# One fused transformer block: head 0's expert indices alone and early, two weight rooms for gathered rows, top-k with 112 sums and 16-bit decoding

## The reference, cut to what matters

```python
q = (xt @ w_query).reshape(T, PEER_HEADS, PEER_KEY_DIM)          # 256 x 8 heads x 256
s1 = einsum('thd,hkd->thk', q[..., :128], sub_keys_1)            # 128 scores a head
s2 = einsum('thd,hkd->thk', q[..., 128:], sub_keys_2)
v1, i1 = lax.top_k(s1, 16); v2, i2 = lax.top_k(s2, 16)
cand = v1[..., :, None] + v2[..., None, :]                       # 16 x 16 sums
top_s, pos = lax.top_k(cand.reshape(..., 256), 16)
eidx = i1[pos // 16] * 128 + i2[pos % 16]                        # 128 experts a token
g = softmax(top_s)
a = gelu(einsum('cd,ced->ce', x, expert_down[eidx]))             # gathered rows of 8 KB
out = einsum('ce,ced->cd', a * g, expert_up[eidx])
```

## Time and profile before

| | |
|---|---|
| three runs | 1957.28, 1952.40, 1950.53 us; median 1952.4 |
| the profiled execution | 1953.55 us, of which the span of the program is 1951.8 |
| busy over the span | PE 93%, DVE 77%, ACT 44%, POOL 29% |
| moved by DMA | 620.26 MB, mean 318 GB/s; gathers 336.11 MB, SP's queue 280.05 MB |
| mean granted clock of PE | 0.979 of full speed |

### The profile page before, as it was taken

The page is one execution under the profiler, slowest core; times in us unless marked ns, Lnnn a source line. Parts: engine busy times, 40 slices in busy tenths (PEclk is TensorE's granted clock), DMA queues, the critical chain, the costliest instruction groups (busy, mean ns, idle before and its releaser), DMA issues.

```text
span 1951.8 us, 26465 instructions
## 1 busy us (share of the span) xinstructions
PE 1814.4 (93%) x10535; PEld 1500.8 (77%) x10535; DVE 1498.7 (77%) x2001; ACT 856.5 (44%) x1262; POOL 566.3 (29%) x369
## 2 busy tenths in 40 slices
PE   8999999999999989979989857679999999999997
PEld 7979987888899879968788744467767776777765
DVE  5354447444456556999999999999989999899888
ACT  4333336444433343323333289864344433344344
POOL 1302300000000000556567668842332113222221
PEclk9999999999999999989999989989999999999999
DMA  7864550355556644899999999989999999999996
GB/s 261 299 226 146 174 170 22 125 179 192 184 182 225 237 162 163 312 426 426 419 426 425 422 372 405 422 362 414 421 426 427 427 427 428 427 428 427 427 427 239
DMA packets 142677, 620.26 MB, mean 318 GB/s; under 512 B 9680, under 2 KB 20192, under 8 KB 84464
## 3 DMA queue, kind: packets, MB, share of 16 engines
q0 software_dynamic: 46352, 336.11, 41.5%
q1 hardware_dynamic: 93712, 280.05, 38.5%
q10 hardware_dynamic: 2512, 2.75, 0.4%
HBM read 616.77 MB, written 2.10 MB: 317 GB/s over the span
## 4 chain that ended last, share of the span: by engine, by line
PE 55%; DVE 23%; DMA 11%; issue 6%; ACT 3%; POOL 1%; SPq 0%; DVEq 0%; ACTq 0%
PE psum L679 54%; DVE down_rows L2306 11%; DMA u_raw<-in_peer_expert_up_dram 10%; POOL down_rows L1359 1%; DVE u_lo L2438 1%; DVE late_sum L2459 1%; ACT u_hi L1814 1%; DVE w_lo L1945 1%; DMA down_rows<-in_peer_expert_down_dram,eidx 1%; DMA x_in<-in_x_dram 0%; PE psum L697 0%; DVE late_rows L2306 0%; DVE onehot L2258 0%; DVE onehot L2261 0%; DVE key L2263 0%
## 5 line engine op out<-in xcount | busy, mean ns | idle before, releaser
L1945 DVE TENSOR_TENSOR w_lo<-raw,w_hi 128x2048 fp32r<-128x2048 f32 x124 | 286.1, 2307 | 337.6 <-ACT w_hi L1460 337.5
L1359 POOL DMA_INDIRECT down_rows<-in_peer_expert_down_dram,eidx x155 | 274.5, 1771 | 630.2 <-DVE eidx L2267 550.5
L1460 ACT CAST w_hi<-raw 128x2048 fp32r<-128x2048 f32 x124 | 236.6, 1908 | 397.4 <-PE psum L679 397.3
L679 PE MATMUL psum<-act_both,w_hi 128*128 128x256 f32 (+1 forms) x1664 | 390.1, 320 | 0.0
L1814 ACT CAST u_hi<-u_raw 128x2048 fp32r<-128x2048 f32 x112 | 214.3, 1913 | 359.7 <-DMA u_raw<-in_peer_expert_up_dram 354.3
L679 PE MATMUL psum<-act_both,w_lo 128*128 128x256 f32 x1088 | 307.0, 282 | 0.0
L679 PEld LDWEIGHTS psum<-act_both,w_hi 128*128 128x128 f32 x1664 | 276.1, 191 | 24.6 <-issue 0.6
L2438 DVE TENSOR_TENSOR u_lo<-u_raw,u_hi 128x2048 fp32r<-128x2048 f32 x112 | 256.5, 2290 | 0.0
L679 PEld LDWEIGHTS psum<-act_both,w_lo 128*128 128x128 f32 x1088 | 207.6, 191 | 0.0
L2306 DVE CUSTOM_DVE_ANT_0 down_rows<-down_rows,xn 128x2048 f32<-128x2048 f32 x91 | 205.4, 2288 | 0.6 <-DVE ind L2216 0.4
L679 PE MATMUL psum<-w_hi,act_both 128*128 128x512 f32 x640 | 201.5, 393 | 0.2 <-DVE w_lo L1945 0.2
(11 more groups left out here) (344 smaller groups left out, 3049.8 us busy)
## 6 DMA issues: line engine op xcount, KB each, us to landing
u_raw<-in_peer_expert_up_dram SPq DMA_DIRECT2D x128, 1024.0 KB, 11.9
raw<-in_w_in_dram SPq DMA_DIRECT2D x76, 1024.0 KB, 5.0
raw<-in_w_out_dram SPq DMA_DIRECT2D x16, 1024.0 KB, 5.0
raw<-in_peer_w_query_dram SPq DMA_DIRECT2D x16, 1024.0 KB, 5.0
raw<-in_w_up_nsa_dram SPq DMA_DIRECT2D x8, 1024.0 KB, 4.9
raw<-in_w_up_fox_dram SPq DMA_DIRECT2D x8, 1024.0 KB, 5.0
cmp_w<-in_k_cmp_w_dram SPq DMA_DIRECT2D x4, 1024.0 KB, 10.7
cmp_w<-in_v_cmp_w_dram SPq DMA_DIRECT2D x4, 1024.0 KB, 10.8
```

Of the source, the lines that this page charges most:

```text
L679: return nc.tensor.matmul(*a, skip_group_check=True, **k)
L1359: nc.gpsimd.indirect_dma_start(rows[:], None, table, bass.IndirectOffsetOnAxis(ap=eidx[:, half, slot:slot + 1], axis=0)).then_inc(landed, 16)
L1460: nc.scalar.copy(w_hi[:, p % 2], raw[:, p]).then_inc(hi_done, 1)
L1945: tt(w_lo[:, p % 2], raw[:, p], f32(w_hi[:, p % 2]), ALU.subtract).then_inc(lo_done, 1)
```

## The change

It has four parts.

- **Two weight rooms for the last blocks.** From block `RAW_PAIR` = 29 on the pieces use `raw[0]` and `raw[1]` only; a load waits for the low part two pieces back. Rooms 2 and 3 become free for gathered rows after block 28, and `order` and `ring` are changed to suit.
- **Head 0 alone.** Its sums and indices come in `topk_end(0, 0, 1)` after the low part of block 29's first piece, head 1's later, after block 30's third. `eidx_done` counts one more; POOL's first 16 slots wait for the first. Lists of heads 2 and 3 move behind the last low part and dot 4, the last `evac` behind dot 5; dots 0 to 2 come earlier.
- **112 sums.** Of the 16 x 16 sums only those of the first 4 rows (all columns) and the first 4 columns of the other 12 are made, two heads in one call.
- **Decoding in 16 bits.** Both lists are compared and multiplied in one operation each over 2 x 16 x 32 elements of 16 bits, followed by one reduction a head; the position is decoded with more small steps.

```diff
+RAW_PAIR = 29
+TOP_A, TOP_B = 4, 4
+NCAND = TOP_A * TOPK + (TOPK - TOP_A) * TOP_B
...
+        def index_sets(t):
+            return 1 if t < TOPK else t // (2 * TOPK) + 2
+        def raw_room(b, p):
+            return p % 2 if isinstance(b, int) and b >= RAW_PAIR else p
...
-        order = [8, 9, 10, 0, 8, 1, 9, 10, 4, 6, 2, 0, 3, 8, 1, 5, 7]
-        ring = [4, 6, 2, 0, 3, 1, 5, 7]
+        order = [8, 9, 10, 2, 3, 8, 9, 10, 4, 6, 0, 2, 1, 3, 8, 5, 7]
+        ring = [4, 6, 0, 2, 1, 3, 5, 7]
...
-                        sp.wait_ge(lo_done, 4 * (b - 1) + p + 1)
-                    sp.dma_start(raw[:, p], src(p)).then_inc(raw_loaded[p], 16)
+                        two = isinstance(b, int) and 4 * b + p >= 4 * RAW_PAIR + 2
+                        sp.wait_ge(lo_done, 4 * b + p - (1 if two else 3))
+                    r = raw_room(b, p)
+                    sp.dma_start(raw[:, r], src(p)).then_inc(raw_loaded[r], 16)
...
-                if slot % (2 * TOPK) == 0:
-                    pool.wait_ge(eidx_done, t // (2 * TOPK) + 1)
+                if t in (0, TOPK) or t and slot % (2 * TOPK) == 0:
+                    pool.wait_ge(eidx_done, index_sets(t))
...
+                elif r < 2:
+                    pool.wait_ge(lo_done, 4 * (NBLK - 1) + r + 3)
                 elif r < 4:
-                    pool.wait_ge(lo_done, 4 * (NBLK - 1) + r + 1)
+                    pool.wait_ge(lo_done, 4 * (RAW_PAIR - 1) + r + 1)
...
-            def top_sums(half, h):
+            def top_sums(half, h0, h1):
+                for c0, rows_, cols_ in ((0, slice(0, TOP_A), TOPK), (TOP_A * TOPK, slice(TOP_A, TOPK), TOP_B)):
+                    nr = rows_.stop - rows_.start
+                    seq(tt(cand[:, at_, c0:c0 + nr * cols_].rearrange("p n (a b) -> p n a b", a=nr),
+                           v1[:, :, rows_].unsqueeze(3).to_broadcast([P, nh, nr, cols_]),
+                           v2[:, :, 0:cols_].unsqueeze(2).to_broadcast([P, nh, nr, cols_]), ALU.add))
...
-                for l in range(2):
-                    seq(tt(oh, pabf[:, l, hs]..., iota, ALU.is_equal))
-                    seq(tt(eq, eq, indf[:, hs, l, :]..., ALU.mult))
-                    seq(V.tensor_reduce(key12[:, l, ks], oh, AX_X, ALU.add))
+                seq(tt(eq, rank16[:, :, 0:ns]..., iota16[:, :, 0:ns]..., ALU.is_equal))
+                seq(tt(eq_h, eq_h, ind16[:, :, :, 0:nh]..., ALU.mult))
+                for h in range(nh):
+                    seq(V.tensor_reduce(key12[:, :, (h0 + h) * TOPK:(h0 + h + 1) * TOPK], ..., AX_X, ALU.add))
...
+            V.tensor_copy(iota16, const("iota").unsqueeze(2).to_broadcast([P, TOPK, 2 * TOPK]))
             lo_piece(QRY0 + 1, 1)
             lo_piece(QRY0 + 1, 2)
             dve.wait_ge(ks_ps, 1)
             top_lists(0, 0)
             lo_piece(QRY0 + 1, 3)
-            top_lists(0, 1)
+            top_sums(0, 0, 1)
 
             lo_piece(QRY0 + 2, 0)
-            top_sums(0, 0)
+            topk_end(0, 0, 1)
             evac(QRY0 + 1)
             lo_piece(QRY0 + 2, 1)
-            top_sums(0, 1)
+            top_lists(0, 1)
             lo_piece(QRY0 + 2, 2)
-            topk_end(0, 0, 2)
+            dot(0)
             lo_piece(QRY0 + 2, 3)
-            dve.wait_ge(ks_ps, 2)
-            top_lists(0, 2)
+            dot(1)
 
             lo_piece(NBLK - 1, 0)
-            top_lists(0, 3)
+            dot(2)
             evac(NBLK - 2)
             lo_piece(NBLK - 1, 1)
-            dot(0)
+            top_sums(0, 1, 2)
             lo_piece(NBLK - 1, 2)
-            dot(1)
-            dot(2)
+            topk_end(0, 1, 2)
             lo_piece(NBLK - 1, 3)
             dot(3)
             dot(4)
+            dve.wait_ge(ks_ps, 2)
+            top_lists(0, 2)
+            top_lists(0, 3)
             dot(5)
+            evac(NBLK - 1)
             dot(6)
-            evac(NBLK - 1)
             topk_weights(1, 0, 0, 2)
```

More of the change, by code:

```diff
@@ L24 @@
 U32 = mybir.dt.uint32
+I16 = mybir.dt.int16
 ALU = mybir.AluOpType
@@ L264, in build @@
         down_rows = [at(f"down_rows{r}", [P, D], kb) for r, kb in enumerate(DOWN_AT)]
-        onehot = at("onehot", [P, 2, TOPK, TOPK], 195)
-        cand = at("cand", [P, 2, TOPK, TOPK], 154)
-        cand2 = at("cand2", [P, 2, TOPK * TOPK], 156)
+        onehot = at("onehot", [P, 2, TOPK, TOPK], 195)[:].rearrange("p l c x -> p (l c x)").bitcast(I16).rearrange(
+            "p (l c x) -> p l c x", l=2, c=TOPK)
+        iota16 = at("iota16", [P, TOPK, TOPK], 197)[:].rearrange("p c x -> p (c x)").bitcast(I16).rearrange(
+            "p (c x) -> p c x", c=TOPK)
+        cand = at("cand", [P, 2, NCAND], 154)
+        cand2 = at("cand2", [P, 2, NCAND], 156)
         list2 = at("list2", [P, 4, NKEYS], 158)
@@ L276, in build @@
         pabf = at("pabf", [P, 2, PEER_H, TOPK], 205)
-        indf = at("indf", [P, PEER_H, 2, TOPK], 206)
+        posf = at("posf", [P, PEER_H, TOPK], 206)
+        rank16 = at("rank16", [P, 2, TOPK], 206.5)[:].rearrange("p l x -> p (l x)").bitcast(I16).rearrange(
+            "p (l x) -> p l x", l=2)
+        ind16 = at("ind16", [P, 2, TOPK], 206.75)[:].rearrange("p l x -> p (l x)").bitcast(I16).rearrange(
+            "p (l c h) -> p l c h", l=2, c=TOPK)
         rT = at("rT", [P, ROUNDS, 4, P], 74)
@@ L509, in build, with uses @@
         SCORE_BANKS = ((2, 3, 6, 7), (4, 5, 6, 7))
-        def uses(b):
+        def index_sets(t):
+            return 1 if t < TOPK else t // (2 * TOPK) + 2
+        def raw_room(b, p):
+            return p % 2 if isinstance(b, int) and b >= RAW_PAIR else p
+        def uses(b, p):
+            if isinstance(b, int) and b >= RAW_PAIR:
+                return RAW_PAIR + 2 * (b - RAW_PAIR) + p // 2 + 1
             return b + 1
@@ L650, in _ @@
             up_v = peer_expert_up[0].rearrange("(c p) d -> p c d", p=P)
-            sp.wait_ge(eidx_done, 8)
+            sp.wait_ge(eidx_done, index_sets(HALVES * SLOTS - 1))
             sp.wait_ge(down_used, SLOTS - len(PE_SLOTS))
@@ L1455, in hi_piece @@
             def hi_piece(b, p):
-                act.wait_ge(raw_loaded[p], uses(b) * 16)
+                r = raw_room(b, p)
+                act.wait_ge(raw_loaded[r], uses(b, p) * 16)
                 if not (isinstance(b, int) and b == 0 and p < 2):
                     act.wait_ge(piece_used, b * 4 + (p - 1))
-                nc.scalar.copy(w_hi[:, p % 2], raw[:, p]).then_inc(hi_done, 1)
+                nc.scalar.copy(w_hi[:, p % 2], raw[:, r]).then_inc(hi_done, 1)
             act.wait_ge(half_sum, 1)
@@ L2226, in top_lists @@
                     V.sem_inc(topk_read, 1)
-            def top_sums(half, h):
-                cd = cand[:, h % 2]
-                seq(tt(cd, val[:, half, h, 0, :].unsqueeze(2).to_broadcast([P, TOPK, TOPK]),
-                       val[:, half, h, 1, :].unsqueeze(1).to_broadcast([P, TOPK, TOPK]), ALU.add))
+            def top_sums(half, h0, h1):
+                nh, at_ = h1 - h0, slice(h0 % 2, h0 % 2 + h1 - h0)
+                v1, v2 = val[:, half, h0:h1, 0, :], val[:, half, h0:h1, 1, :]
+                for c0, rows_, cols_ in ((0, slice(0, TOP_A), TOPK), (TOP_A * TOPK, slice(TOP_A, TOPK), TOP_B)):
[3 more added lines that the diff above has]
+                           v2[:, :, 0:cols_].unsqueeze(2).to_broadcast([P, nh, nr, cols_]), ALU.add))
                 settle()
-                top16([(cd.rearrange("p a b -> p (a b)"), cand2[:, h % 2, :], top[:, half, h, :], pos[:, half, h, :])])
+                top16([(cand[:, h % 2, :], cand2[:, h % 2, :], top[:, half, h, :], pos[:, half, h, :])
+                       for h in range(h0, h1)])
                 settle()
@@ L2242, in topk_end @@
                 g = gw[half][:, hs]
-                tt(g, top[:, half, hs], top[:, half, hs, 0:1].to_broadcast([P, nh, TOPK]), ALU.subtract).then_inc(soft_in, 1)
+                ins = tt(g, top[:, half, hs], top[:, half, hs, 0:1].to_broadcast([P, nh, TOPK]), ALU.subtract)
+                if h1 % 2 == 0:
+                    ins.then_inc(soft_in, 1)
                 if half == 1 and h0 == 0:
                     dve.wait_ge(numT_done, 1)
-                seq(ts(pab[:, 0, hs], pos[:, half, hs], 4, None, ALU.logical_shift_right))
-                seq(ts(pab[:, 1, hs], pos[:, half, hs], 15, None, ALU.bitwise_and))
-                seq(V.tensor_copy(indf[:, hs], ind[:, half, hs]))
+                at_ = pos[:, half, hs]
+                seq(ts(pab[:, 0, hs], at_, 4, None, ALU.logical_shift_right))
+                seq(ts(pab[:, 1, hs], at_, 2, None, ALU.logical_shift_right))
+                seq(V.tensor_copy(posf[:, hs], at_))
+                seq(V.tensor_copy(ind16[:, :, :, 0:nh].rearrange("p l c h -> p h l c"), ind[:, half, hs]))
                 settle()
@@ L2251, in topk_end @@
                 settle()
[L2252 to L2255, removed]
-                ks = slice(h0 * TOPK, h1 * TOPK)
-                for l in range(2):
[L2258 to L2262, removed]
```

(30 more changed lines are left out.)

4 lines of the change are left out of this document (2 added, 2 removed).

## The result

The changed kernel takes 1965.05 us (median; 1961.70 to 1969.24), the kernel before 1952.40 (1950.53 to 1957.28): ratio 1.0061, 95% interval 1.0044 to 1.0078. It is 12 us slower, in the forecast's direction and 6 us dearer than the 1959 that was forecast. That lies inside the outer range (1950 to 1966) but above the forecast case's own (1955 to 1963); of the rivals it is nearest to E, all terms at their dear end, 1965.5. The profiled execution has a span of 1965.1 against 1951.8, +13.3.

A forecast was written before the change was run, and what follows sets the result against it. DMA transfers were taken to set the pace from first gather to expert_up's last chunk, the Vector engine second. Terms -1.3 + 8.1 = +6.8 gave 1960.4 profiled, 1959 beside the runs; own range 1955 to 1963, outer 1950 to 1966.

The forecast's parts named there:

- outer range: Whole kernel: 1950 to 1966 us, from rival D to rival E, leaving out rival C and a part of rival E.
- forecast case: Whole kernel: start and pairs -1.3 us, room used twice +8.1, giving 1959; own range 1955 to 1963, chance 0.50.
- rival E: Whole kernel, all terms at their dear end: stall 9, decoding 5.95, drain 10; +13 us, 1965.5; chance 0.09.
- check on the earlier trace: Start: weight and gather packets alternate one for one; 1.65 us at 0.39 each gives the five weight packets seen.
- the load of block 30's first piece: Start: issued about 784.1, slowed 9.8 us by gathers, lands at 798.9; TensorE stalls 5.6 us, then 1.3 more.
- Rival B: Start: weight loads keep their rate beside gathers, no stall, 3.5 us less: 1956; chance 0.11.
- Rival A2: Top-k per pair: 16-bit steps run at twice the rate, decoding 4.9, some 2 us less: 1957; chance 0.14.
- the -1.3: Start of the second half: eighth dot 12.7 us later, sums save 17.0, 3.0 given back in waits.
- I cost this at nothing: Start: TensorE's first row product waits for the later copy of queries; costed at nothing, 3 us if not.
- The drain: End: gather 142 must wait for dot 141, both in room 1; cost 8.1 us, bounds 7 and 10.
- rival D: End: the room-1 wait is hidden by rows in hand; -1.3 us, 1951; chance 0.07.
- Rival C: Gather stage: the 13 us of lead carry through since DMA bounds it; -6 us, 1946; chance 0.09.

The follow-up runs named there:

- e_hold: Changed kernel with e_ring's room list, every gather held until block 30's last low part, dots 0 to 2 moved behind it: 1964.03 us, ratio 1.0058.
- e_four: Changed kernel with the four raw weight rooms, room order and ring of the kernel before; head 0 alone and new top-k stay: 1947.83 us, ratio 0.9976.
- e_ring: Changed kernel with fixed room list (3, 7, 6, 0, 2, 1), so gather 142 no longer takes gather 141's room: 1955.09 us, ratio 1.0014.
- e_four_copy: e_four with the copy of block 30's queries moved ahead of head 3's lists and dot 5 on DVE: 1946.68 us, ratio 0.9970.
- e_diag: e_four_copy with the first two diagonal dots of TensorE's rows moved ahead on DVE: 1948.03 us, ratio 0.9976 to the kernel before.
- e_ring_diag: e_ring with the copy of queries and the first two diagonal dots moved ahead on DVE: 1956.37 us, ratio 1.0014 to the kernel before.
- e_same_room_before: Kernel before with fixed room list (3, 7, 6, 2, 0, 1), so gathers 141 and 142 share room 3: 1963.09 us, ratio 1.0053.
- e_topk_before: Kernel before with only the new top-k (112 sums, 16-bit decoding), heads 0 and 1 still together: 1945.56 us, ratio 0.9965.

## Why the prediction was right, and where it was short

Right: the direction, the place of both losses, and that neither is hidden. By the ratios the steps from kernel to kernel are top-k -6.8, head 0 alone with its order on DVE +2.1, the pair of raw rooms with its gathers +7.4, the double room +9.2. They add to +11.9 by the way they are formed, each from its neighbour; each is uncertain by some 2.5 to 4 us, so the +2.1 can't be told from nothing. All dear terms came together, as in rival E (chance 0.09): its stall of 9, drain of 10 and decoding of 5.95 measured 9.4, 9.2 and 5.70.

- **The start.** The first gather (776.0 for 776.1), the one-for-one alternation and the price of one load hold: 5.0 + 9.8 = 14.8 forecast, 15.2 and 16.9 measured. (The forecast's check on the earlier trace rows was looser than it says: 1.65 / 0.39 is 4.2 packets, not five.) One failed step is which load is first: "the load of block 30's first piece". The load ahead of it, for block 29's last piece, goes out at 778.5 and meets the same gathers; the forecast took it as landed. So there is one gap of TensorE, 7.07 us up to 798.07, where two of 5.6 and 1.3 between 797 and 811 were forecast; that their sum agrees is luck. The other failed step is a term that the sum doesn't have: behind the gap TensorE ran for a while at the lower clock, 2.1 us. Together TensorE is 9.4 late where the forecast had 7, and the eighth dot stands at 840.35 for 838.1. e_hold shows that the meeting is the cause, e_four that two rooms more cover it. Rival B falls. Its price, 3.5 for a stall of 7, is worked out nowhere and was too low: from e_four to e_ring, which has the stall, A grows by 8.3 and the time by 7.4, nearly one for one.
- **Per pair.** Sums are right to 0.03. Decoding was put in the middle of two guesses and is 5.70. Rival A2's mechanism is right: compare and multiply run at twice the rate. Its 4.9 is wrong, because the reductions got dearer: 1.96 us for two, where it had 1.33, and the small steps take 2.3 for 2.1. The Trainium skill, page "VectorE: DVE Perf Modes", section on the perf-mode tier table, gives this split for bf16, twice the rate for a tensor_tensor and none gained for a reduction. The trace agrees for both (0.69 for 1024 elements; no gain in a reduction) and adds the loss.
- **Up to the second half.** With the measured terms: +15.0 for the eighth dot, -7 x 2.46 for sums, +6 x 0.24 for decoding make -0.8; it came at +2.7, so 3.5 are left over for waits, for 3 forecast. Of the 4.0 by which the -1.3 was short, 2.3 are the later eighth dot (in the main the lower clock), 1.4 the decoding, 0.5 the waits, and the sums give 0.2 back. "I cost this at nothing" for the late copy of queries held: e_four_copy, e_diag and e_ring_diag move it and win nothing that can be told.
- **The end.** The drain is 9.2 for 8.1, inside the bounds of 7 and 10: gather 142 lands 5.4 us after its issue, not 5.9, but 143 takes 3.7 more instead of 2.46, and the ten behind it 2.50 each. e_ring and e_same_room_before leave nothing of rival D.
- **Rival C.** e_four has the lead without the stall: its first gather goes at 774.3, and that of e_topk_before at 786.2. It is not faster (+2.1 by the ratios, inside the two intervals). So 12 us of lead carry nothing to the end here. That it is DVE which can't use them fits its 39 busy us of 40. It has more to do as well: head 0 alone is decoded in 775.63 - 771.39 = 4.24 us and head 1 in 4.25 (kernel after), together 2.8 more than the 5.70 of a pair. No run here made DVE faster at the start alone, so this last step is argued, not shown.
- **Behind the last dot** 1.4 us came that no term holds. A single profile can't tell them from chance.

## What to carry to other kernels

When rooms are renumbered, print for each transfer the one that last used its room, across every seam between two lists: one repeated number drained an in-order queue for 9 us in two kernels. A buffer that seems spare may be the slack that hides slow transfers; before it is given away, price every load in flight, not only the first that is wanted late, at the rate it gets beside the new traffic. Test the parts of a bundled change alone: here one was worth 7 us, and the others cost 19.

## What the runs showed of the hardware

- Two DMA queues share an engine by packets, not bytes: 462 packets of weights and 491 of gathers in 14 us, 0.93 MB and 3.63 MB. A 1 MB load, alone in 4.8 to 5.7 us (e_hold), took 15.2 and 16.9 beside gathers.
- Behind 7.07 us without work TensorE's granted clock was 0.60 and then 0.72 in two stretches of 5 us, and a group of three products took 0.64 us for 0.36: the gap cost 2.1 us beyond itself.
- DVE in 16 bits: compare and multiply of 1024 elements took 0.69 us each. A single head's multiply of 512 also takes 0.69, its compare 0.42: there the index factor has an innermost dimension of one element and is repeated over the next. The Trainium skill, page "VectorE: DVE Perf Modes", section "Mode 2×_1P — pack two bf16 into one 32-bit read", asks for 16-bit operands with a step of one. The two times fit that, and int16 goes at the rate that the page gives for bf16.
- A reduction of 512 int16 elements took 0.96 to 1.07 us, one of 512 elements in 32 bits 0.69. It reads with a stride, which the one before did not; whether width or stride costs it wasn't separated.
